# Forget gates' sums enter the attention scores by one fp32r product of 128 rows instead of two fp32 products of four rows

## The reference

```python
q, k, v, f = jnp.split(p_fox, [hd, 2 * hd, 3 * hd], axis=-1)
log_f = jax.nn.log_sigmoid((f + b_forget).astype(jnp.float32)).transpose(0, 2, 1)
...
c = jnp.cumsum(log_f, axis=-1)
...
s = jnp.einsum('bhqd,bhkd->bhqk', qb, k).astype(jnp.float32) * scale
return s + cb[..., :, None] - c[..., None, :]
```

## Time and profile before

| | |
|---|---|
| median of 3 runs | 2535.82 us (2534.22 to 2537.2) |
| the profiled execution: time | 2531.52 us |
| its span, first to last instruction | 2529.7 us |
| mean granted clock of TensorE | 0.925 of full speed |
| TensorE busy | 2222.8 us, 88% of the span |
| VectorE busy | 1155.4 us, 46% |
| ScalarE busy | 809.3 us, 32% |
| moved by DMA | 545.14 MB, mean 215 GB/s |

### The profile page before, as it was taken

One profiled execution on the slowest core, in us unless ns is written; L12 is line 12 of the kernel. 1 busy time (PEld: TensorE's weight loads), 2 busy tenths in 40 slices (PEclk: granted clock), 3 DMA queues, 4 the chain that ended last, 5 costly groups with the idle time before them and its releaser, 6 DMA issues.

```text
span 2529.7 us, 29586 instructions
## 1 busy us (share of the span) xinstructions
PE 2222.8 (88%) x10942; PEld 1533.1 (61%) x10942; DVE 1155.4 (46%) x1587; ACT 809.3 (32%) x1057; POOL 234.6 (9%) x263
## 2 busy tenths in 40 slices
PE   5888869999588985999949989979989989898998
PEld 4675444443467544343327877768867868676787
DVE  2654450000465446000045565465565566667455
ACT  2343120001234322000023343443333335494433
POOL 4000011110000001232110010010010010001000
PEclk8988979999798897999979999889989989999999
DMA  9736729998473573999955545345545545324553
GB/s 178 254 121 215 263 109 405 409 408 343 159 251 123 195 266 160 400 413 416 393 181 172 187 132 189 100 157 183 183 158 181 180 132 182 119 93 131 181 184 116
DMA packets 213823, 545.14 MB, mean 215 GB/s; under 512 B 25084, under 2 KB 40540, under 8 KB 188224
## 3 DMA queue, kind: packets, MB, share of 16 engines
q1 hardware_dynamic: 187456, 507.74, 56.0%
q0 software_dynamic: 18320, 22.55, 3.7%
q10 hardware_dynamic: 7920, 13.18, 1.4%
HBM read 611.92 MB, written 13.25 MB: 247 GB/s over the span
## 4 chain that ended last, share of the span: by engine, by line
issue 43%; PE 18%; DMA 4%; DVE 2%; POOL 2%; ACT 1%; POOLq 1%; DVEq 1%; ACTq 0%; SPq 0%
PE ps L1318 3%; PE ps L514 2%; PE ps L515 2%; PE ps L516 2%; PE ps L1341 2%; PE ps L1354 1%; DMA moe_w<-in_w 1%; POOL rs L2468 1%; PE ps L1031 1%; PE ps L1376 1%; DMA ring<-in_ada_w 1%; DMA proj<-in_w 1%; PE ps L1303 1%; POOLq L2467 1%; PE ps L1996 0%
## 5 line engine op out<-in xcount | busy, mean ns | idle before, releaser
L492 DVE TENSOR_TENSOR w_lo<-ring,w_hi 128x2048 fp32r<-128x2048 f32 (+4 forms) x232 | 502.8, 2168 | 525.2 <-ACT w_hi L485 481.0
L485 ACT CAST w_hi<-ring 128x2048 fp32r<-128x2048 f32 (+4 forms) x232 | 419.0, 1807 | 724.6 <-PE ps L516 628.4
L514 PE MATMUL ps<-w_hi,XTh 128*128 128x512 f32 (+4 forms) x1328 | 522.5, 393 | 34.5 <-DVE w_lo L492 14.9
L515 PE MATMUL ps<-w_lo,XTh 128*128 128x512 f32 (+4 forms) x1328 | 513.4, 387 | 0.0
L516 PE MATMUL ps<-w_hi,XTl 128*128 128x512 f32 (+4 forms) x1328 | 512.5, 386 | 0.0
L514 PEld LDWEIGHTS ps<-w_hi,XTh 128*128 128x128 f32 x1328 | 257.3, 194 | 98.9 <-DVE w_lo L492 13.9
L516 PEld LDWEIGHTS ps<-w_hi,XTl 128*128 128x128 f32 x1328 | 256.4, 193 | 51.8
L515 PEld LDWEIGHTS ps<-w_lo,XTh 128*128 128x128 f32 x1328 | 257.6, 194 | 47.8
L514 PE MATMUL ps<-w_hi,hTh 128*128 128x512 f32 x320 | 124.9, 390 | 0.0
L516 PE MATMUL ps<-w_hi,hTl 128*128 128x512 f32 x320 | 124.7, 390 | 0.0
L515 PE MATMUL ps<-w_lo,hTh 128*128 128x512 f32 x320 | 124.6, 389 | 0.0
(11 more groups left out here) (522 smaller groups left out, 3001.7 us busy)
## 6 DMA issues: line engine op xcount, KB each, us to landing
moe_w<-in_w SPq DMA_DIRECT2D x144, 1024.0 KB
ring<-in_ffn_w SPq DMA_DIRECT2D x128, 1024.0 KB, 5.1
ring<-in_ada_w SPq DMA_DIRECT2D x72, 1024.0 KB, 6.4
proj<-in_w SPq DMA_DIRECT2D x48, 1024.0 KB
ring<-in_w_in SPq DMA_DIRECT2D x24, 1024.0 KB, 6.9
ring<-in_mb_w_in SPq DMA_DIRECT2D x20, 1024.0 KB, 5.2
ring<-in_ml_w_in SPq DMA_DIRECT2D x12, 1024.0 KB, 5.3
ring<-in_w_out SPq DMA_DIRECT2D x8, 1024.0 KB, 5.6
```

What stands on the lines that cost most here:

```text
L485: nc.scalar.copy(w_hi[:, i, 0:n], ring[:, j, 0:n]).then_inc(hi_ready, 1)
L492: nc.vector.tensor_tensor(w_lo[:, i, 0:n], ring[:, j, 0:n], w_hi[:, i, 0:n].bitcast(F32), ALU.subtract).then_inc(raw_used, 1)
L514: nc.tensor.matmul(out, sh, mh, start=start, stop=False)
L515: nc.tensor.matmul(out, sh, ml, start=False, stop=False)
```

## The change

The running sums are now produced on all 128 partitions at once. VectorE clears `gate_w` (128 x 2 x 128) and writes the negative logarithms into its columns 0 to 3, 32 to 35, 64 to 67 and 96 to 99, the first two sets with factor -8 on the positive softplus and the last two with 8. The product with `cum` therefore has 128 stationary columns, and gives four groups of rows: 8c, 8c, -8c, -8c. `forget_rows` rounds all of it to fp32r (`gate_rows`), and in the second and fourth group puts the remainder, PSUM less rounded value. So the first 64 partitions hold the high and low parts of 8c, the other 64 those of -8c.

`head_rows_steps`, new at j = UKV between `stick_z(3)` and `heads_of_latents`, builds the other operand `head_rows` (128 x 4 heads x 256). In partitions 0 to 63 it is one on the head's rows and zero elsewhere (from `of_head`, columns of the identity), in partitions 64 to 127 it is -8c on the head's rows and zero elsewhere. After that the upper half of `gate_rows` is overwritten with ones. The product of `gate_rows` and `head_rows[:, f, :]` is then 8c at the query less 8c at the key, in one call with 128 rows, in place of two with four. The three new buffers lie in `Y`, which is not in use then, and `of_head` is 128 x 4.

```diff
--- before.py
+++ after.py
@@ -285,6 +285,11 @@
         row_base = sb("row_base", [P, L, 4])
         part_weight = sb("part_weight", [96, 1])
         half = sb("half", [P, 24])
+        of_head = sb("of_head", [P, 4])
+
+        gate_w = Y[:, :, :].rearrange("p t d -> p (t d)")[:, 0:NT * P].rearrange("p (t c) -> p t c", t=NT)
+        gate_rows = at("gate_rows", [P, S], F32R, Y_at + 4 * NT * P)
+        head_rows = at("head_rows", [P, 4, S], F32R, Y_at + 4 * (NT * P + S))
         y_row = ctx.enter_context(nc.sbuf_tensor("y_row", [P, 2, NT], mybir.dt.int32))
         small = sb("small", [P, 12, 64])
         lse = sb("lse", [P, 5, 8])
@@ -1655,7 +1660,7 @@
                 if j == 4:
                     pe.wait_ge(dve_did, t.dve_step.at(4))
                     for tt in range(NT):
-                        last = nc.tensor.matmul(ps[0:4, 6, 0:S], small[:, 6, 4 * tt:4 * tt + 4], cum[:, tt, :],
+                        last = nc.tensor.matmul(ps[:, 6, 0:S], gate_w[:, tt, :], cum[:, tt, :],
                                                 start=(tt == 0), stop=(tt == NT - 1))
                     last.then_inc(pe_did, 1)
                 elif j == 5:
@@ -1768,6 +1773,11 @@
 
             def forget_steps():
                 dve.wait_ge(params_ready, 1)
+                dve.wait_ge(ident_loaded, 16)
+                nc.vector.memset(gate_w, 0.0)
+                for g in range(4):
+                    at_ = slice(32 * g, 32 * g + 32)
+                    nc.vector.tensor_copy(of_head[at_, :], ident[at_, 32 * g:32 * g + 4])
                 u = small[:, 0, 0:8].rearrange("p (t h) -> p t h", t=NT)
                 TT(u, proj[:, :, FOX + 768:FOX + 772], b_forget[:, l, :].unsqueeze(1).to_broadcast([P, NT, 4]), ALU.add)
                 dve.drain()
@@ -1775,7 +1785,13 @@
                 dve.drain()
                 t.add(dve_step=2, act_step=1)
                 softplus_vector(dve, t, 8)
-                TS(small[:, 6, 0:8], small[:, 5, 0:8], -1.0, None, ALU.mult).then_inc(dve_did, 1)
+
+                for g in range(2):
+                    for tt in range(NT):
+                        to = gate_w[:, tt, 64 * g:64 * g + 64].rearrange("p (a c) -> p a c", a=2)[:, :, 0:4]
+                        last = TS(to, small[:, 5, 4 * tt:4 * tt + 4].unsqueeze(1).to_broadcast([P, 2, 4]),
+                                  8.0 * (2 * g - 1), None, ALU.mult)
+                last.then_inc(dve_did, 1)
                 TS(rs[:, 0, 0:2], small[:, 7, 0:2], 1.0 / DQ, 1e-6, ALU.mult, ALU.add)
                 TS(rs[:, 0, 2:4], small[:, 7, 2:4], 1.0 / DKV, 1e-6, ALU.mult, ALU.add)
                 dve.drain().then_inc(mean_ready, 1)
@@ -1792,8 +1808,21 @@
             def forget_rows():
                 dve.wait_ge(pe_did, t.pe_step.at(1))
                 t.add(pe_step=1)
-                TS(rowT[0:4, 0, :], ps[0:4, 6, 0:S], 8.0, None, ALU.mult)
-                TS(rowT[0:4, 1, :], ps[0:4, 6, 0:S], -8.0, None, ALU.mult).then_inc(forget_read, 1)
+                nc.vector.tensor_copy(gate_rows[:, :], ps[:, 6, 0:S])
+                dve.drain()
+                for p0 in (32, 96):
+                    at_ = slice(p0, p0 + 32)
+                    last = TT(gate_rows[at_, :], ps[at_, 6, 0:S], gate_rows[at_, :].bitcast(F32), ALU.subtract)
+                last.then_inc(forget_read, 1)
+
+            def head_rows_steps():
+
+                dve.drain()
+                nc.vector.tensor_copy(head_rows[0:64, :, :], of_head[0:64, :].unsqueeze(2).to_broadcast([64, 4, S]))
+                TT(head_rows[64:128, :, :], gate_rows[64:128, :].bitcast(F32).unsqueeze(1).to_broadcast([64, 4, S]),
+                   of_head[64:128, :].unsqueeze(2).to_broadcast([64, 4, S]), ALU.mult)
+                dve.drain()
+                nc.vector.tensor_copy(gate_rows[64:128, :], ones[64:128, 0:1].to_broadcast([64, S]))
 
             def heads_of_latents():
                 projected(dve, t)
@@ -1843,6 +1872,7 @@
                 elif j == UKV:
                     stick_z(2)
                     stick_z(3)
+                    head_rows_steps()
                     heads_of_latents()
                     STT(sb_sp, sb_z, -1.0, sb_z, ALU.mult, ALU.max).then_inc(dve_did, 1)
                     t.add(dve_step=1)
@@ -1999,10 +2029,7 @@
                         f = HEADS[i]["forget"]
                         if f is not None:
                             out = ps[:, scores_bank(i), c0:c0 + nk]
-                            pick = ident[0:4, f:f + 1]
-                            nc.tensor.matmul(out, rowT[0:4, 0, tt * P:(tt + 1) * P],
-                                             pick.to_broadcast([4, nk]), start=False, stop=False)
-                            last[i] = nc.tensor.matmul(out, pick.to_broadcast([4, P]), rowT[0:4, 1, 0:nk],
+                            last[i] = nc.tensor.matmul(out, gate_rows[:, tt * P:(tt + 1) * P], head_rows[:, f, 0:nk],
                                                        start=False, stop=True)
                 for i in both:
                     last[i].then_inc(scores_ready, 1)
```

## The result

| | changed | before |
|---|---|---|
| median, 10 runs each, on one chip | 2524.63 us (2508.22 to 2541.02) | 2536.51 us (2531.6 to 2542.54) |
| ratio | 0.9944, 95% interval 0.9921 to 0.9968 | |
| the profiled execution: time, span | 2522.17, 2520.4 us | 2531.52, 2529.7 us |

By the ratio the changed kernel is faster by 0.56%, some 14 us (0.0056 x 2536.5), and the interval goes from 8 to 20 us; the medians differ by 11.9 us. The forecast was 2519.5 with a range of 2511 to 2527.5. Against the median of 2535.8 that it started from, that is a ratio of 0.9936, inside the interval.

A forecast was written before the change was run, and what follows sets the result against it. TensorE alone bounds the forgetting heads' scores, 15.17 us a layer, 11.4 of it gates' products. -17.9 + 1.8 + 0 = -16.1 us: 2535.8 to 2519.7, stated as 2519.5, range 2511 to 2527.5.

The forecast's parts named there:

- Term 1: Gates' products in the four forgetting heads' scores: 16 pairs of calls become 16 fp32r calls, -17.9 us.
- Rival D: Gates' products: fp32r with 128 rows streams no faster than float32, 8.4 us saved, 2527.5; chance 0.05.
- rival E: Ada stream or expert weights end last whatever TensorE does, gain turns into DMA waits: 2535.8; chance 0.05.
- The sign of E: Longer DMA waits in front of the ada products in the changed profile would show the forecast wrong; no size given.
- rival B: Clock comes back inside the shortened block, work behind it runs faster: 2.3 us a layer, 2515; chance 0.24.
- A: The forecast itself, block of the forgetting heads at the low clock: 2519.5, own range 2516 to 2523; chance 0.50.
- The low end of the range: Whole kernel: lower cost of the products takes 3.6 us off, a clock that comes back 4.6 more, 2511.3.
- Term 2: Gates' sums: small operations in `forget_steps`, longer first load, `forget_rows`; 0.92 us a layer, +1.8 us, bounds 1.0 and 2.6.
- Term 3: `head_rows_steps` on VectorE: 2.7 us, covered, so costed at 0; with no cover 5.4 us.
- rival C: `head_rows_steps` not covered, copies dearer or a late L492 moves ACT's next conversion: +5.4 us, 2525; chance 0.12.
- The wait at `turn(0)`: First use in the block: exponentials ready at about 5.3 us, needed at 6.2, so no wait, under 1 us to spare.
- rival F: Stretch 208.5 to 264 stays at the low clock through another order of gaps: slower, up to near 2567; chance 0.04.

The follow-up runs named there:

- four-row fp32r calls: The kernel before, its two four-row products in fp32r instead of float32, low parts left out of the result: 2525.56 us, ratio 0.9939.
- Products twice: The kernel before with each pair of four-row products issued twice, on rows scaled by 4 in place of 8: 2557.96 us, ratio 1.0078.
- second trace: The changed kernel again, unchanged, on another chip: 2521.28 us, ratio to before 0.9923.
- third trace: The changed kernel once more, unchanged: 2523.26 us, ratio to before 0.9936.
- the preparation alone: The changed kernel's new preparation, but two plain float32 four-row products on the high parts, low parts left out: 2545.73 us, ratio to before 1.0024.
- the pieces moved: The changed kernel with `forget_rows` behind the turned vectors' copies and `head_rows_steps` behind the expert weights' parts on VectorE: 2522.2 us, ratio to before 0.9918.

## Why the prediction was right

The forecast said 2519.5 and faster with 0.91. On three chips the ratio was 0.9944, 0.9923 and 0.9936, which on medians of 2536.5, 2540.2 and 2540.8 is 14, 20 and 16 us; the sum of the terms was 16.1. The steps bear it out; that the number came within 2 to 5 us is partly luck, since each interval is some 6 us wide on either side, and since two things left out of the sum, a clock that comes back and longer waits for ada pieces, pull in opposite directions.

**Term 1, -17.9 us.** Right for a block at the low level: 6.32 us where 6.2 was said, 15.17 - 6.32 = 8.85 us a layer, 17.7 for both (17.9 said). The groups cost 0.62 and 0.72 us (0.51 and 0.71 said); it is the small one that is dearer, and the four-row fp32r calls show why: 128 columns cost 0.21 us there, as 256 do, where 0.11 was taken. That a call of 128 columns costs half of one of 256 was the wrong part of the term. The change-over was 0.72 - 2 x 0.21 = 0.30 us in the large group, as said (0.29), but 0.62 - 2 x 0.21 = 0.20 in the small one, which takes back half of that error; 0.1 us a small group is left. Rival D (2527.5) is out, since a float32 pair of 256 columns has 1.06 us at the full level and the fp32r pair 0.43. Products twice shows that the block is on the path to the end with nothing beside it, which rival E (2535.8) denied. The sign of E, longer waits for ada pieces, did come: 8.3 and 9.4 us in the two layers of the first changed trace against 5.2 and 6.6, but 6.6 and 6.7 in the second and 7.5 and 6.7 in the third. Even the first, 5.9 us more in all, is far from the 16 that E needed, and the kernel with the products twice has them too.

**The clock, rival B.** The forecast let the block stay at 0.50. That was so in seven blocks of ten. In the three others it came back, as B had it, and the block took 4.7 us: 1.6 us less in it. The 96-row scores behind it took 1.3 us less than in before (188.57 - 187.25 against 2.6), but 0.7 less than in the second trace of the changed kernel (2.0 us), where the clock came back just there. Against a block that stays low that is the 2.3 us a layer that B had. What A and B both had wrong is that they were set against one another as outcomes of the kernel. Each is an outcome of a block in an execution. The low end of the range, 2511, adds B to a cost of term 1 that has the full clock in it already, so it counts a part of it twice.

**Term 2, +1.8 us.** The four small operations take 99.76 - 99.46 = 0.30 us where one took 0.09, +0.21 (0.27 said). `forget_rows` costs +0.72 us on VectorE and +0.74 on TensorE's path (0.55 said), near the upper bound, where the pieces don't overlap. The memset and the four copies are covered as said: VectorE's wait for ACT behind them is 3.90 us in layer 0 of the changed kernel and 4.68 in before. The 0.1 us for the first load is shown by no run.

**Term 3, 0.** Right: 2.30 us on VectorE (2.7 said), and at the same clock the stretch that holds it takes 53.00 us with it and without it. Moving it to a later place brought nothing either, so rival C (2525) is out.

**The wait at `turn(0)`.** The forecast had it fit with under 1 us to spare. It fits in the 6.3 us blocks, and with the clock back TensorE waits 0.40 us.

**Behind the block, rival F.** The table has the changed kernel at -23.6 us at 879 and at -16.5 at 964, which looks like a gain given back. Most of it isn't. The kernel with the preparation alone and the one with the products twice lose 4.6 and 3.6 us in that stretch too, and their blocks of layer 1 are no shorter. The windows of this one stretch of like work, in before, in products twice, in preparation only and in the changed kernel:

```profile
878.70:964.40 85.70, 68.66 (x372) 39.28 (x369) 40.89 (x82) 22.38 (x45) 3.48 (x3) 0.92 0.81 295
```

```profile
903.30:992.60 89.30, 70.80 (x372) 39.94 (x369) 40.91 (x82) 22.34 (x45) 4.07 (x3) 0.88 0.80 287
```

```profile
883.30:973.60 90.30, 72.05 (x372) 40.38 (x369) 40.99 (x82) 23.12 (x48) 3.45 (x3) 0.87 0.79 284
```

```profile
855.10:947.90 92.80, 73.14 (x372) 40.86 (x369) 40.98 (x82) 23.12 (x49) 4.22 (x3) 0.85 0.78 282
```

The same instructions take 85.7 us at a clock of 0.92 in before, and 89.3 to 92.8 at 0.88 to 0.85 in the others. So some 4 us of the 7 are the luck of the one trace of before. All nine other traces in the table lose 2.5 to 8.4 us in that stretch. The mechanism of F, more time at the low level behind the block, exists, but it moved traces with an old block as well, and not by the 16 us that it needed. Whether the other 3 us in the trace of the changed kernel belong to the change isn't known: its third trace has 8.4 at a clock of 0.83, its second 4.5 at 0.89. Chance of this kind is also why the first profile is only 9.4 us faster than that of before where the medians differ by 12 and more: the profiled execution of before, 2531.5, lies 5 us under its median of 2536.5, and that of the changed kernel 2.5 us under its own.

**What stays open.** Why the preparation alone measured +6 us when its steps account for some 1.8: the interval reaches down to 0.5, and the trace puts the rest in stretches where the clock differs. Whether a kernel with the pieces moved is faster than the changed one (0.9918 and 0.9936) isn't settled. What in an execution decides the clock inside the block isn't either, nor whether the longer waits for ada pieces cost anything at the end.

## What to carry to other kernels

Where TensorE runs alone for many microseconds, small products of plain float32 on a few rows are the first place to look: fp32r with high and low parts cost 0.73 us of TensorE's time a layer here, for the copy and subtraction on VectorE, and took their groups from 2.00 and 3.69 us to 0.62 and 0.72. Read such a gain at the granted clock of its place, and leave the gain or loss of a clock that comes back as a case for each execution and no term of the sum. Lay more than one trace of a kernel beside another before a "gain given back" gets a cause, and don't take work out if the data behind it choose how much other work there is: double it with scaled operands instead.

## What was not expected of the hardware

- TensorE stayed at 0.50 for the whole of 182 to 207 us, busy for 25.00 us of 25, with half-height and four-row float32 products, and in the preparation-only kernel it fell from 1.00 to 0.50 at about 188 us in the midst of them, with no gap. The Trainium skill, "TensorE: Matmul & The Clock Gate", Part 1, says that keeping TensorE busy lifts the throttle. These rows don't agree with it. The block of the changed kernel's layer 0 agrees with it: it had 1.00 after 183.5 us. Seven others with 128-row products of fp32r were at 0.50 from end to end, so full height alone doesn't settle it.
- The clock is low before the block begins. In all 24 blocks of the twelve traces TensorE had just stood still for 3.49 us, waiting for VectorE, and the clock fell within 1.2 us of the end of this wait. In layer 0 of before:

```profile
177.45 0.70 PE L1642 MATMUL ps<-temp,later 128*128 128x256 f32 x2 [3.49 <-DVE temp L1862]
```

  Whether the block would run at 1.00 without the wait was not tried.
- A four-row fp32r call takes 0.21 us from start to start at the low level for 128 columns and for 256. Two of full height take 0.62 and 0.72 us, with the change-over of the array's shape in it.
- The same block has either clock within one execution: 4.69 us in layer 0 and 6.32 in layer 1 of the third trace.
